# Expert weights in 1 MB transfers: splitting every refill of a ring in two

## The chip, the cores and the metric

The kernel runs on one core of a Trainium2 chip. Its time is device microseconds of one execution; the median of three runs of the kernel before is 2060.9 us (2057.89 to 2061.14). Weights and activations are float32.

## The reference, cut to what matters

Two blocks are applied to 256 tokens of width 1024. The first mixes a long convolution and a gated recurrence and ends in a retrieval of single-neuron experts. The second has two layers, each with attention (or spatial gating) and then sixteen experts of which each token takes two. The change lies in the experts of the two layers:

```
def expert_block(args):
    xblk, e = args
    return (jax.nn.silu(xblk @ w_gate[e]) * (xblk @ w_up[e])) @ w_down[e]
```

with `w_gate`, `w_up` and `w_down` of 1024 x 1024 float32 for each of 16 experts: 12 MiB an expert, 192 MiB a layer, all of it read once.

## The kernel before

The program is a row of stages: `front_stage` (the first block), `gating_stage` (layer 0's mixing), `moe_stage` for layer 0, `dilated_stage` (layer 1's attention) and `moe_stage` for layer 1. What matters here is `moe_stage`.

The sixteen experts are taken as eight pairs, and one pair is a visit. A visit of TensorE packs the tokens of the pair's two experts (up to 64 each), multiplies by gate (two halves of the columns), up (two halves) and down (two halves), and scatters the result back into PSUM. The two experts share the 128 rows of the output: expert j of the pair writes rows 64 j to 64 j + 63. Each of the six steps has a contraction of eight chunks of 128, and its weights come in two pieces of four chunks. So a visit takes 12 pieces (`HALVES`), and a layer 96. One piece is 128 partitions x 16 KB = 2048 KB (2.097 MB), and holds for both experts four chunks by 512 columns. TensorE does 16 matmuls of 512 columns on it.

The pieces live in a ring of 12 slots (`MOE_SLOTS`, `AHEAD`, `RING`). The first eleven are loaded during the stage before, the twelfth at the start of `moe_stage`. All others are refills: piece s goes into slot s mod 12 when TensorE has finished with piece s - 12. SP issues them all, in the order of use, from `load` (line 2558): it waits for `s_step`, which TensorE raises by one after the last matmul of every piece (line 2686), and calls `moe_load` (line 2459), which issues the transfer (line 2463). Each slot has a semaphore in `s_w`; TensorE waits for it ahead of the first matmul of a piece (`step`, line 2679). All transfers of SP stand in one hardware queue.

`IN_TWO` is the number of the first piece that comes in two transfers: chunks 0 and 1 of the piece (`QUARTER` = 2) in the first, 2 and 3 in the second, each with 8 KB of contiguous bytes for each partition. The second half has semaphores of its own, `s_w_rest`, for which TensorE waits in the middle of the piece (line 2681). Before, only the last eight pieces of a layer do so.

Behind the last piece SP issues the parameters of the closing norm and, in layer 0, three weights of the next stage (`w_v`, `w_k`, `w_in1`, line 2586); the first thing that TensorE does with them is `value_job` (line 2010 in the rows), at the end of layer 0's stage. All loops over visits are unrolled; a second pass, for experts with over 64 tokens, is a loop that is skipped when no expert has so many. The eighth visit is a function of its own (`visit_last`), behind a value that is loaded at run time. The semaphores of a stage are cleared by GpSimd at the start of the next (`clear_stale`).

Of the kernel before, what the change touches and what calls it, by code (L numbers as in the profile page):

```python
# [25 lines left out]
DC = D // P  # L26
# [1965 lines left out]
def dilated_weights(K):  # L1992

    return [K.cut(moe_base(K, slots), P, DC, w) for slots, w in ((3, N_DH * HD), (5, N_DH * HD), (7, N_DH * HD + MEM_W))]
# [451 lines left out]
HALVES = 2 * len(MOE_STEPS)  # L2446
# [7 lines left out]
def moe_slot(K, i):  # L2454

    return K.cut(moe_base(K, i + 1), P, DC // 2, 2, 512)


def moe_load(K, sp, layer, i, pair, chunks=slice(0, DC // 2)):

    name, h = MOE_STEPS[i // 2]
    src = K.dram[name][layer * NE + pair * 2 + h:layer * NE + pair * 2 + h + 1, :, i % 2, :]
    return sp.dma_start(moe_slot(K, (pair * HALVES + i) % MOE_SLOTS)[:, chunks],  # L2463
                        src.rearrange("o p (c j n) -> p (o c) j n", j=2, n=512)[:, chunks])


def moe_stage(K, layer):
# [9 lines left out]
    def sem(name):  # L2477
        return K.sem(f"moe{layer}_{name}")

    C = PACK_ROWS  # L2480
    PAIRS = NE // 2
    STEPS = MOE_STEPS
    NS = len(STEPS)
    AHEAD = MOE_SLOTS
    LAPS = [len(range(k, PAIRS * HALVES, AHEAD)) for k in range(AHEAD)]
    IN_TWO = PAIRS * HALVES - 8
    QUARTER = DC // 4

    at = Room(moe_base(K, AHEAD), ROUTE_COLS + 2 * T + 2 * MEM_W)
# [17 lines left out]
    FIRST_FREE = PAIRS * HALVES - (AHEAD - 3)  # L2507

    s_w = K.s_moe_w
    s_w_rest = [sem(f"w{s % AHEAD}_rest_in") for s in range(IN_TWO, PAIRS * HALVES)]  # L2510
    s_par, s_np, s_cols = K.lasting_sem(f"moe{layer}_params_in"), sem("passes"), sem("norm_columns_in")
    s_pk, s_pg, s_xm, s_xe, s_step, s_sg, s_h = (sem(n) for n in (
        "pack", "pack_gated", "xe_mm", "xe", "step_mm", "silu", "hidden"))
# [9 lines left out]
    def since(eng, s, count):  # L2523

        if not (isinstance(count, int) and count <= 0):
            eng.wait_ge(s, count)

    def visits(eng, body, prologue=None, behind=None):

        pairs = PAIRS - 1 if behind else PAIRS

        def one_pass(q, before_last=None):
            if prologue:
                prologue(q * PAIRS)
            for e in range(pairs):
                if before_last and e == pairs - 1:
                    before_last()
                body(q, e)  # L2540

        def load():
            eng.wait_ge(s_np, 1)
            loaded.append(eng.value_load(NPASS[0:1, 0:1], min_val=1, max_val=PASSES))  # L2544

        loaded = []
        one_pass(0, load)
        passes = loaded[0]
        with eng.If_ne(eng.lower_val(passes - 1), 0):
            with eng.Fori(1, passes) as q:  # L2550
                if behind:
                    behind(q - 1)
                one_pass(q)

    with nc.Block() as block:  # L2555
        @block.sync
        def _(sp):
            def load(q, e):
                for i in range(EARLY_SLOTS if isinstance(q, int) and e == 0 else 0, HALVES):
                    s = e * HALVES + i  # L2560
                    if isinstance(q, int) and s < AHEAD:
                        moe_load(K, sp, layer, i, e).then_inc(s_w[s], 16)
                        continue
                    used = s - AHEAD if s >= AHEAD else s + (LAPS[s] - 1) * AHEAD - PAIRS * HALVES
                    since(sp, s_step, q * (PAIRS * HALVES) + (used + 1))
                    if s < IN_TWO:
                        moe_load(K, sp, layer, i, e).then_inc(s_w[s % AHEAD], 16)
                    else:
                        moe_load(K, sp, layer, i, e, slice(0, QUARTER)).then_inc(s_w[s % AHEAD], 16)
                        moe_load(K, sp, layer, i, e, slice(QUARTER, DC // 2)).then_inc(s_w_rest[s - IN_TWO], 16)  # L2570

            if not last_layer:
                sp.dma_start(LNT, d["ln2_cols"]).then_inc(s_cols, 16)
            visits(sp, load)
            more = sp.value_load(K.NMORE[0:1, 0:1], min_val=0, max_val=PASSES - 1)
            sp.wait_ge(s_step, more * (PAIRS * HALVES) + (PAIRS * HALVES - (AHEAD - 1 - PARAM_SLOT)))
            sp.dma_start(LG, d["ln2_g"][layer].partition_broadcast(P)).then_inc(s_par, 16)
            sp.dma_start(LB, d["ln2_b"][layer].partition_broadcast(P)).then_inc(s_par, 16)

            if not last_layer:  # L2580
                steps = sp.value_load(NSTEPS[0:1, 0:1], min_val=FIRST_FREE, max_val=FIRST_FREE + (PASSES - 1) * (PAIRS * HALVES))
                names = ("w_v", "w_k", "w_in1")
                for n, (to, name, later) in enumerate(zip(dilated_weights(K), names, (0, 2, 4))):
                    sp.wait_ge(s_step, steps + later if later else steps)
                    src = d[name].rearrange("(c p) n -> p c n", p=P) if n == 2 else d[name][0].rearrange("p (c n) -> p c n", c=DC)
                    sp.dma_start(to, src).then_inc(K.s_att_w[n], 16)
            if last_layer:
                for t in range(TT):
                    sp.wait_ge(s_fin, t + 1)
                    sp.dma_start(K.out[t * P:(t + 1) * P, :], H[:, t, :]).then_inc(s_out, 16)  # L2590
                sp.wait_ge(s_out, 16 * TT)
# [61 lines left out]
        def _(te):  # L2653
# [19 lines left out]
            def step(q, e, i, operand, b, s_op, used, part=range(DC)):  # L2673

                for c in part:
                    s = e * HALVES + 2 * i + c // (DC // 2)
                    if c % (DC // 2) == 0:
                        te.wait_ge(s_op, used + (c // (DC // 2) + 1))
                        te.wait_ge(s_w[s % AHEAD], q * (LAPS[s % AHEAD] * 16) + (s // AHEAD * 16 + 16))
                    if c % (DC // 2) == QUARTER and s >= IN_TWO:  # L2680
                        te.wait_ge(s_w_rest[s - IN_TWO], q * 16 + 16)
                    for j in range(2):
                        x = pe.matmul(bank[b][j * C:(j + 1) * C, :], operand[:, c, j * C:(j + 1) * C],  # L2683
                                      RING[s % AHEAD][:, c % (DC // 2), j, :], start=(c == 0), stop=(c == DC - 1))
                    if c % (DC // 2) == DC // 2 - 1:
                        x.then_inc(s_step, 1)
# [15 lines left out]
            def gate_and_up(q, e):  # L2702
                n = q * PAIRS + e
                since(te, s_ye, n * 2)
                step(q, e, 0, XE, 0, s_xe, n * 2)
                if e:
                    te.wait_ge(s_pgt, n)
                    for h in range(2):
                        add_back(n - 1, h)
                step(q, e, 1, XE, 1, s_xe, n * 2)  # L2710
                since(te, s_pgt, n)
                since(te, s_ht, n * 2)
                for i in range(2, 4):
                    step(q, e, i, XE, i, s_xe, n * 2)
# [145 lines left out]
def moe_stage_0(K):  # L2860
    moe_stage(K, 0)


def moe_stage_1(K):
    moe_stage(K, 1)
# [195 lines left out]
```

## Time and profile before

| | |
|---|---|
| median of 3 runs | 2060.9 us |
| the profiled execution | 2064.71 us |
| its span (first to last instruction) | 2062.8 us |
| mean granted TensorE clock | 0.935 |
| TensorE busy | 1768.5 us (86%) |
| VectorE busy | 776.9 us (38%) |
| DMA | 761.82 MB, mean 369 GB/s |
| expert matmuls, L2683 | 3072, 680.3 us busy, 42.2 us idle before them |

A row "from-to" of the windows gives each engine's busy time with the number of instructions, then the granted clock, the mean share of the 16 DMA engines that is busy, and what they moved. In a row of the timeline the first number is the start, the second the length of a group of like instructions that follow on each other, and the bracket tells the idle time before it and what ended it. Since the ends of matmuls are modelled, gaps of some tenths of a microsecond are to be read as order, not as exact times. Layer 0's expert stage runs from about 1049 to 1483 us of the span, layer 1's from about 1619 us to the end.

### The profile page before, as it was taken

To read this page: it belongs to the slowest core of one execution; us is meant where nothing else is said; L and a number is where in the kernel's file an instruction comes from. 1 tells how busy PE (TensorE), PEld (TensorE's weight loads), DVE (VectorE), ACT (ScalarE), POOL (GpSimd) and SP (SyncE) were. 2 spreads that over 40 slices of the span, in tenths; PEclk is the share of its full clock that TensorE was granted. 3 is DMA by queue.
4 is the path that set the end of the run, shared out by engine and by line. 5 is a ranking of instruction groups with operands and counts; after the bars stand their busy time and mean duration, and the time that the engine had idled before them with its cause. 6 is when DMAs were issued, how large, how long until landed. Compare 5 with 4: busy or idle time off the path is not lost. (4 is left out here: it accounts for less than half of the span.)

```text
span 2062.8 us, 23546 instructions
## 1 busy us (share of the span) xinstructions
PE 1768.5 (86%) x9356; PEld 918.0 (44%) x9356; DVE 776.9 (38%) x1897; ACT 424.3 (21%) x1000; POOL 299.9 (15%) x284
## 2 busy tenths in 40 slices
PE   9999997876655665568999999988899999999887
PEld 7779873552321111124564444333377644433332
DVE  3945178776667777754230000000224300000002
ACT  2481122221221122223111101000223200000001
POOL 0000033543444444430000000000000000000000
PEclk9999998898887667889999999999999999999999
DMA  7237389999999999997789999999964999999997
GB/s 267 93 125 302 143 341 404 397 421 421 420 421 421 421 421 421 421 421 304 315 356 426 426 428 426 428 426 423 420 242 199 378 428 426 427 426 427 426 424 310
DMA packets 81710, 761.82 MB, mean 369 GB/s; under 512 B 9060, under 2 KB 10053, under 8 KB 18102
## 3 DMA queue, kind: packets, MB, share of 16 engines
q1 hardware_dynamic: 43926, 489.35, 56.9%
q0 software_dynamic: 37664, 270.84, 31.9%
q8 instruction: 78, 1.28, 0.2%
q14 instruction: 42, 0.34, 0.0%
HBM read 759.11 MB, written 1.05 MB: 369 GB/s over the span
## 5 line engine op out<-in xcount | busy, mean ns | idle before, releaser
L2683 PE MATMUL bank<-arena 128*64 128x512 f32 x3072 | 680.3, 597 | 42.2 <-DMA arena<-in_w_up 16.8
L1085 PE MATMUL bank<-arena 64*64 64x512 f32 x2032 | 320.4, 784 | 224.4 <-ACT arena L795 224.4
L2683 PEld LDWEIGHTS bank<-arena 128*64 128x64 f32 x3072 | 231.0, 137 | 477.5 <-issue 448.2
L588 POOL DMA_INDIRECT arena<-in_peer_uv,arena x256 | 288.5, 1127 | 614.2 <-PE bank L1085 301.0
L1458 DVE CUSTOM_DVE_ANT_0 arena<-arena 128x1024 f32<-128x1024 f32 x256 | 313.6, 1225 | 156.6 <-DMA arena<-in_peer_uv,arena 153.2
L2811 DVE TENSOR_TENSOR arena<-arena,bank 128x512 f32<-128x512 f32 x32 | 22.0, 687 | 705.7 <-PE bank L2683 705.7
L1085 PEld LDWEIGHTS bank<-arena 64*64 64x64 f32 x2032 | 92.6, 175 | 432.5 <-ACT arena L795 257.0
L844 PE MATMUL bank<-arena 128*128 128x272 f32 (+2 forms) x768 | 144.8, 349 | 0.2 <-ACT arena L614 0.2
L844 PEld LDWEIGHTS bank<-arena 128*128 128x128 f32 x768 | 126.2, 191 | 19.4 <-issue 2.5
L790 ACT ACTIVATE arena<-arena 128x4 f32<-128x4 f32 (+1 forms) x69 | 14.1, 205 | 465.0 <-DVE arena L1458 465.0
L1541 POOL DMA_DIRECT2D arena<-in_w_router x2 | 1.1, 574 | 566.0 <-POOLq L2555 531.3
L2616 ACT ACTIVATE arena<-bank 128x512 f32<-128x512 f32 x32 | 19.1, 597 | 277.9 <-PE bank L2670 165.1
L795 ACT ACTIVATE arena<-arena 128x64 f32<-128x64 f32 x256 | 68.6, 336 | 25.1 <-DVE arena L1476 25.1
L2610 ACT ACTIVATE arena<-bank 128x512 f32<-128x512 f32 x32 | 19.0, 595 | 240.9 <-PE bank L2692 240.9
L2625 ACT ACTIVATE arena<-bank 128x512 f32<-128x512 f32 x32 | 19.1, 597 | 216.7 <-PE bank L2683 216.7
L2670 PE MATMUL bank<-arena 128*128 128x512 f32 x128 | 59.7, 606 | 3.0 <-ACT arena L2625 3.0
L2661 PE MATMUL bank<-arena,h_res 128*128 128x128 f32 x512 | 62.1, 281 | 0.0
L2661 PEld LDWEIGHTS bank<-arena,h_res 128*128 128x128 f32 x512 | 60.9, 199 | 0.0
L1005 PE MATMUL bank<-arena 128*128 128x128 f32 x512 | 59.8, 275 | 0.0
L1005 PEld LDWEIGHTS bank<-arena 128*128 128x128 f32 x512 | 58.5, 192 | 0.0
L2229 PE MATMUL bank<-arena 128*128 128x256 f32 x224 | 51.2, 382 | 0.0
L2229 PEld LDWEIGHTS bank<-arena 128*128 128x128 f32 x224 | 41.6, 190 | 7.0 <-issue 1.3
(466 smaller groups left out, 1538.0 us busy)
## 6 DMA issues: line engine op xcount, KB each, us to landing
arena<-in_w_gate SPq DMA_DIRECT2D x64, 2048.0 KB, 32.3
arena<-in_w_up SPq DMA_DIRECT2D x56, 2048.0 KB, 32.4
arena<-in_w_down SPq DMA_DIRECT2D x56, 2048.0 KB, 33.2
arena<-in_w_in SPq DMA_DIRECT2D x13, 2048.0 KB, 8.2
arena<-in_w_up SPq DMA_DIRECT2D x16, 1024.0 KB, 38.8
arena<-in_w_down SPq DMA_DIRECT2D x16, 1024.0 KB, 27.0
arena<-in_w_out SPq DMA_DIRECT2D x2, 4096.0 KB, 18.2
arena<-in_wq SPq DMA_DIRECT2D x3, 2048.0 KB, 12.4
```

What stands on the lines that cost most here:

```text
L588: nc.gpsimd.indirect_dma_start(SLOT[slot_of[j]], None, d["peer_uv"], bass.IndirectOffsetOnAxis(IDX[:, u % 4, k:k + 1], 0)).then_inc(s_row[ ...
L795: a.activation(DIAG[:, k, :], DIAG1, ACT.Copy, scale=WGT[:, u, k:k + 1]).then_inc(s_diag, 1)
L844: m = pe.matmul(bank[n % 2][:, 0:w], RING[b % 2][:, c, q * P:(q + 1) * P], NT[:, c, lo:lo + w], start=(c == 0), stop=(c == DC - 1))
L1005: m = pe.matmul(bank[b][:, j * P:(j + 1) * P], WQ_CHUNK[k][c][:, j * P:(j + 1) * P], XT[t][:, c, :], start=(c == 0), stop=(c == DC - 1))
L1085: m = pe.matmul(bank[banks[t][half]][to:to + HALF, :], DIAG[lo:lo + HALF, k + j, :], row[lo:lo + HALF, D + half * 512:D + (half + 1) * 512 ...
L1458: v.tensor_tensor_reduce(SLOT[slot_of[j]][:, 0:D] if n == 0 else SCR, SLOT[slot_of[j]][:, 0:D], XF[u // PH], 1.0, 0.0, ALU.mult, ALU.add, ...
L2229: m = pe.matmul(b[:, 0:T], (WK if kind == "k" else WIN)[:, c, cols], XT[:, c, :], start=(c == 0), stop=(c == DC - 1))
L2616: a.activation(HID[:, b * 512:(b + 1) * 512], bank[b][:, :], ACT.Silu).then_inc(s_sg, 1)
L2661: x = pe.matmul(bank[c // 4][:, c % 4 * P:(c % 4 + 1) * P], H[:, t, c * P:(c + 1) * P], PK[:, t, :], start=(t == 0), stop=(t == TT - 1))
L2670: pe.matmul(bank[Y_BANKS[t][h]][:, :], PGT[:, t * P:(t + 1) * P], HID[:, h * 512:(h + 1) * 512], start=isinstance(n, int) and n == 0, stop ...
L2683: x = pe.matmul(bank[b][j * C:(j + 1) * C, :], operand[:, c, j * C:(j + 1) * C], RING[s % AHEAD][:, c % (DC // 2), j, :], start=(c == 0), ...
L2811: v.tensor_tensor(HID[:, cs], HID[:, cs], bank[2 + b][:, :], ALU.mult).then_inc(s_h, 1)
```

## The change

`IN_TWO` becomes 12: every piece from the thirteenth on (s >= 12, that is every refill) comes in two transfers of 1024 KB. The first twelve of each layer stay whole. The second halves get one semaphore for each slot, twelve instead of eight in a stage, and since a slot is now refilled in seven laps, TensorE waits for a count that grows by 16 with each lap.

```
-    IN_TWO = PAIRS * HALVES - 8
+    IN_TWO = AHEAD
...
-    s_w_rest = [sem(f"w{s % AHEAD}_rest_in") for s in range(IN_TWO, PAIRS * HALVES)]
+    s_w_rest = [sem(f"w{s}_rest_in") for s in range(AHEAD)]
...
                         moe_load(K, sp, layer, i, e, slice(0, QUARTER)).then_inc(s_w[s % AHEAD], 16)
-                        moe_load(K, sp, layer, i, e, slice(QUARTER, DC // 2)).then_inc(s_w_rest[s - IN_TWO], 16)
+                        moe_load(K, sp, layer, i, e, slice(QUARTER, DC // 2)).then_inc(s_w_rest[s % AHEAD], 16)
...
                     if c % (DC // 2) == QUARTER and s >= IN_TWO:
-                        te.wait_ge(s_w_rest[s - IN_TWO], q * 16 + 16)
+                        te.wait_ge(s_w_rest[s % AHEAD], q * ((LAPS[s % AHEAD] - 1) * 16) + s // AHEAD * 16)
```

## Rows read from the trace of the kernel before

**Rows 1.** The page's 40 equal slices of the span (51.6 us each).
```profile
DMA  7237389999999999997789999999964999999997
GB/s 267 93 125 302 143 341 404 397 421 421 420 421 421 421 421 421 421 421 304 315 356 426 426 428 426 428 426 423 420 242 199 378 428 426 427 426 427 426 424 310
```

**Rows 2.** The chain of waits from 1000 us on: start, us, what.
```profile
1708.53 13.97 PE bank L2683 x64
...
1759.54 13.97 PE bank L2683 x64
...
1883.91 49.00 DMA arena<-in_w_gate
...
1942.24 49.61 DMA arena<-in_w_gate
...
2020.21 27.67 DMA arena<-in_w_down
```

**Rows 3.** Timeline of TensorE in layer 1's seventh visit, whole pieces (start, us, what).
```profile
1952.76 3.65 PE L2683 MATMUL bank<-arena 128*64 128x512 f32 x16 [0.40 <-DMA arena<-in_w_up]
...
1967.47 3.65 PE L2683 MATMUL bank<-arena 128*64 128x512 f32 x16 [1.25 <-DMA arena<-in_w_up]
```

**Rows 4.** Windows: whole pieces in the first row, halves in the other two.
```profile
1650.00:1850.00 200.00, 196.94 (x952) 80.55 (x950) 11.33 (x39) 19.78 (x36) 0.00 (x0) 1.00 1.01 427
1438.00:1466.00 28.00, 27.05 (x126) 8.90 (x122) 2.67 (x4) 2.07 (x4) 0.00 (x0) 1.00 1.01 419
2008.00:2022.00 14.00, 14.00 (x68) 4.66 (x66) 0.69 (x1) 0.60 (x1) 0.00 (x0) 1.00 1.01 421
```

**Rows 5.** Timeline of SP's queue in layer 1: its first refills.
```profile
1628.64 10.63 SPq L2463 DMA_DIRECT2D arena<-in_w_gate  x4
```

**Rows 6.** Line 2463 from 1550 us on: all its expert loads, issue to landing.
```profile
DMA to landing us min/median/max: 7.1/32.8/51.6
```

**Rows 7.** Timeline of TensorE in layer 1's last visit, halves.
```profile
2006.86 19.26 PE L2683 MATMUL bank<-arena 128*64 128x512 f32 x88
2026.65 1.94 PE L2683 MATMUL bank<-arena 128*64 128x512 f32 x8 [0.53 <-DMA arena<-in_w_up]
...
2036.56 1.94 PE L2683 MATMUL bank<-arena 128*64 128x512 f32 x8 [0.46 <-DMA arena<-in_w_down]
...
2045.54 1.94 PE L2683 MATMUL bank<-arena 128*64 128x512 f32 x8 [0.67 <-DMA arena<-in_w_down]
2047.92 1.94 PE L2683 MATMUL bank<-arena 128*64 128x512 f32 x8 [0.44 <-DMA arena<-in_w_down]
```

**Rows 8.** Timeline of TensorE: end of layer 0's seventh visit, last visit, `w_v`.
```profile
1417.02 3.65 PE L2683 MATMUL bank<-arena 128*64 128x512 f32 x16 [0.54 <-DMA arena<-in_w_down]
1424.46 8.78 PE L2683 MATMUL bank<-arena 128*64 128x512 f32 x32 [3.79 <-issue]
...
1456.56 1.94 PE L2683 MATMUL bank<-arena 128*64 128x512 f32 x8 [0.45 <-DMA arena<-in_w_up]
...
1464.15 1.94 PE L2683 MATMUL bank<-arena 128*64 128x512 f32 x8 [0.29 <-DMA arena<-in_w_down]
1466.54 1.94 PE L2683 MATMUL bank<-arena 128*64 128x512 f32 x8 [0.45 <-DMA arena<-in_w_down]
...
1471.15 7.32 PE L2683 MATMUL bank<-arena 128*64 128x512 f32 x32
...
1487.85 5.43 PE L2010 MATMUL bank<-arena 128*128 128x384 f32 x16 [2.23 <-DMA arena<-in_w_v]
```

**Rows 9.** Windows: the gather of the first block.
```profile
500.00:900.00 400.00, 240.90 (x1412) 86.19 (x1410) 286.49 (x668) 85.19 (x258) 179.42 (x157) 0.79 1.01 421
```

**Rows 10.** SP's issues, ns min/median/max: room in the queue; then layer 1's end.
```profile
L2463 SPq DMA_DIRECT2D arena<-in_w_down x4: 327/328/328, 1142.2 to 1152.5; - x4
L2463 SPq DMA_DIRECT2D arena<-in_w_down x8: 2129/2140/3832, 2001.6 to 2020.2; - x8
```

**Rows 11.** DMA issues of the page: KB each, median us from issue to landing.
```profile
arena<-in_w_down SPq DMA_DIRECT2D x16, 1024.0 KB, 27.0
```

## The prediction

> **What bounds the kernel now.** I read the page's slices first [rows 1]. In the two expert stages (slices 22 to 29 and 33 to 39) the DMA engines are busy for nine tenths or more, at 420 to 428 GB/s. TensorE is busy for 86% of the whole span, so the shares alone don't say which of them sets the end. The chain of waits does [rows 2]: from 1883.9 us on it consists of two spans of 49.0 and 49.6 us on a `w_gate` transfer and one of 27.7 us on a `w_down` transfer, between them only a little TensorE work, which ends as TensorE starts on the last half piece. Before 1883.9 us the chain is TensorE's own, since eleven pieces lie ready when the stage starts. TensorE takes 51.0 us for a visit of twelve pieces (1708.53 to 1759.54 in the same rows), while the DMA engines need 12 x 4.9 = 58.9 us for twelve, with 4.9 us from the spacing below. So TensorE gains some 8 us on the transfers in every visit, eats up the ring, and in the sixth visit starts to wait.
>
> The spacing: where TensorE waits for whole pieces it restarts at 1952.76 and, three pieces later, at 1967.47 us [rows 3], 4.90 us for each, though the work on one takes 3.65 us. One piece is 2048 KB or 2.097 MB; at 4.905 us that is 427.5 GB/s, which agrees with the 427 GB/s of a long stretch [rows 4]. The DMA share there is 1.01: all 16 engines are full, nothing idles between transfers.
>
> Does this bind from the first refill to the end? SP issues the first refill of layer 1 at 1628.64 us [rows 5] and TensorE starts on the last half piece at 2047.92 us [rows 7]: 419.3 us for 84 pieces. 84 x 4.905 is 412.0 us. The missing 7 us are the start from an empty queue (the shortest time from issue to landing in this stage is 7.1 us [rows 6], 2.2 us more than one piece takes) and hold-ups of single engines. One of these can be seen: from 2036.56 to 2045.54 us three half pieces land in 8.98 us, 3.0 us each, where the next is 2.4 behind [rows 7]. So the stage's end is first refill + 84 pieces x time of one + a fixed tail of some 15 us, and what the change does to the time of a piece counts in full.
>
> **What the change does.** Pieces 12 to 87 of each layer (76 of the 84 refills) become two transfers of 1024 KB with rows of 8 KB per partition instead of one with rows of 16 KB; the first twelve and the last eight stay as they are. It removes no byte, no matmul and no wait.
>
> *Time of a transfer.* The last eight pieces of either layer already run in this form, so its price stands in the trace. In layer 0 TensorE restarts on a half at 1456.56 and, four landings later, at 1466.54 us [rows 8]: 2.495 us for each, 4.99 us for a piece. In layer 1 it is 2026.65 to 2036.56 us [rows 7]: 2.478, or 4.955 for a piece. The DMA rate over stretches with only such transfers in them is 419 and 421 GB/s beside 427 for whole pieces, at the same DMA share of 1.01 [rows 4]; with 420 that gives 2.097/0.420 - 2.097/0.427 = 0.08 us more per piece (0.07 to 0.09 by the two). The restarts give 0.05 and 0.085. A third witness from another queue: the gather of the first block, in 8 KB rows too, runs at 421 GB/s [rows 9]. I take 0.08 us. 76 x 0.08 = 6.1 us for a layer, 12.2 us for both; the bounds are 2 x 76 x 0.05 = 7.6 and 2 x 76 x 0.09 = 13.7 us.
>
> The Trainium skill would give other sums. "SBUF — State Buffer", section "The DMA setup-cost knee", puts a 1 MiB transfer at 341 GB/s because each pays some 2 us of its own; I weigh it as a rival below. "DMA: Bandwidth & Descriptors", section "Why small descriptors are slow", names about 3 cycles per packet on the engine's internal bus. Eight packets more per engine and piece at the 850 MHz that the page gives for the fabric would be 0.03 us, an estimate of some 4 us for the whole change: a third of what the trace shows for the same step.
>
> *SP.* 152 more transfers to issue. One takes 0.33 us of SP in a stretch where the queue has room [rows 10], two 0.66 us, against one piece released per 3.5 us at TensorE's fastest: hidden. Later the queue is full and an issue of a half is held for 2.1 us, most of the time of one landing [rows 10]. The median from issue to landing is 32.8 us over all loads of layer 1 and 27.0 us for the halves of `w_down` [rows 6, 11], so with halves less lies in the queue, but still some ten transfers (27.0/2.49). It doesn't run dry. Behind the blocked SP wait only the norm parameters and, in layer 0, `w_v`, `w_k` and `w_in1`, which stand in the same queue behind the pieces anyway.
>
> *TensorE.* It gets 76 waits in a layer in the middle of pieces, each ahead of a matmul. Their price where they are already satisfied: from 2006.86 us 88 matmuls run in 19.26 us over three such waits [rows 7], 0.219 us each, and 64 without any take 13.97 us [rows 2], 0.218 each. So nothing. Where they aren't satisfied, TensorE starts a piece one half landing (2.5 us) earlier, finishes it some 1.8 us earlier (half of the 3.65) and releases its slot that much sooner; SP is blocked then and the queue full, so the next landing is not moved. Behind TensorE's wait stand ScalarE's and VectorE's steps of the visit, which only come when the pieces do.
>
> *What is late next.* At the end of layer 0 TensorE is close to even with the transfers: it waits 0.29 and 0.45 us on the halves of one piece, runs the last two pieces in one go (32 matmuls from 1471.15 us), and then waits 2.2 us for `w_v`, which stands behind the last piece in the queue [rows 8]. With every landing 6 us later both are late by 6 us; TensorE, which doesn't get slower, has 6 us of slack in this visit. From there to layer 1's first refill the order is TensorE's own and shifts as a whole. In layer 1 it waits before each of the last two halves (0.67 and 0.44 us), so the later landings pass on entirely.
>
> *Four semaphores more in a stage* are cleared by GpSimd at the start of the next, which is otherwise idle there: nothing.
>
> **Sum.** The profiled execution is 2064.7 us (span 2062.8 and 1.9 around it), 3.8 above the median of the three timed runs. It would become 2064.7 + 12.2 = 2076.9; the median 2060.9 + 12.2 = 2073.1, 0.6% slower.
>
> **Rivals.**
> 1. *The rate of 419 to 421 GB/s belongs to the end of a layer and not to the size* (parameters and other small queues run there). Then 1 MB transfers in the middle of a layer run at 427 and nothing changes: 2061. For it: all direct rows come from the ends. Against it: the rate is down from the first half piece on, and the gather of another stage has it.
> 2. *The finer grain gains* (the other side). The place is the border from the seventh to the last visit: the seventh ends on a piece that TensorE waited for (1417.02 us, 3.65 us of work [rows 8]); with halves it would end 1.8 us sooner, then comes a gap of 3.79 us and the last visit, in layer 0 with hardly a wait. If the last visit is TensorE's there, 1.8 us are gained in each layer: 2060.9 - 3.6 = 2057.3. It decides only if the halves cost less than 1.8/76 = 0.024 us a piece; the rows say three times that, and the waits of 0.29 to 0.67 us in both last visits say that the landings rule.
> 3. *Extra hold-ups.* More transfers and instructions bring more delays like the 1.5 us (8.98 less 3 x 2.49) in [rows 7]. They add up where they hit the engine that is already last. Two more in each layer: 2060.9 + 12.2 + 6 = 2079.
> 4. *Each half pays its completion anew.* If the 2.2 us of start (7.1 less 4.9) came with each of the 152 additional transfers, it would be 334 us: 2395. The halves in [rows 7, 8] that land 2.4 to 2.5 us apart, with all 16 engines full, speak against it. By the 341 GB/s of the Trainium skill ("SBUF — State Buffer", same section) a piece would take 6.15 us and the kernel an estimated 190 us more; the 419 to 421 GB/s of [rows 4] are this very size, so the trace disagrees: transfers that stand in a queue don't pay it one by one.
> 5. *The small price only* (some 4 us, 2065): a cost per packet less than what the ends show.
>
> **How the numbers follow.** My forecast has 82%. Rival 1 has 5%, rival 2 3%, rival 3 7%, rival 4 1%, rival 5 2%. What a measurement of this kernel can tell from no change is about 0.2%, 4 us, so below 2056.8 is faster and above 2065.0 slower. The forecast, rivals 3 and 4 and half of rival 5 are slower: 91%; rival 1 and half of rival 5 are the same, and I leave rival 2 its 3% for faster: 6% and 3%. The range goes from the lower bound, 2060.9 + 7.6 = 2068.5, less 1 for the spread of the three runs (2057.9 to 2061.1), to the upper, 2060.9 + 13.7 = 2074.6, plus two extra hold-ups of 1.5: 2067.5 to 2077.6.
>
> **What would show it.** Right: about 420 GB/s through both expert stages at a share of 1.01; TensorE's waits in the sixth and seventh visit in halves, 2.49 us apart; the first refill of layer 0 at the same time as now, that of layer 1 some 6 us later, the last half landing some 12 us later; the first wait for a transfer in a layer earlier than now. Wrong: 427 GB/s with 8 KB rows (rival 1), a last visit with no wait for a transfer (rival 2), stretches below 410 GB/s or a DMA share under 1.0 between refills (rivals 3 and 4).

## The result and the profile after

The changed kernel takes 2074.16 us in the median (2071.93 to 2078.91) against 2060.9 us; the ratio is 1.0062 with a 95% interval of 1.0047 to 1.0077, so it is slower by 10 to 16 us. Forecast were 2073.1 us and a range of 2067.5 to 2077.6.

First two windows of the kernel after, one in the middle of each layer; the second is the first stretch of [rows 4]. The columns are PE, PEld, DVE, ACT and POOL busy, then granted clock, DMA share and GB/s.

```profile
1100.00:1280.00 180.00, 177.46 (x842) 70.65 (x844) 9.71 (x31) 16.22 (x30) 0.00 (x0) 1.00 1.01 420
1650.00:1850.00 200.00, 196.94 (x952) 80.70 (x950) 11.35 (x39) 19.78 (x36) 0.00 (x0) 1.00 1.01 420
```

The same stretch of layer 0 in the kernel before:

```profile
1100.00:1280.00 180.00, 177.01 (x840) 70.22 (x838) 9.17 (x31) 16.62 (x30) 0.00 (x0) 1.00 1.01 427
```

Where the kernel before moved 427 GB/s at a DMA share of 1.01 (this row and [rows 4]), this one moves 420 at the same share. The DMA engines are as full as before and get less done.

The stages' ends, from SP's and TensorE's timelines of the kernel after: the first refill of layer 0, the first matmul on `w_v`, the first refill of layer 1, and the last matmuls of layer 1 (L2670, the scatter of the last result).

```profile
1056.72 11.40 SPq L2463 DMA_DIRECT2D arena<-in_w_gate  x8
...
1492.14 5.43 PE L2010 MATMUL bank<-arena 128*128 128x384 f32 x16 [0.77 <-DMA arena<-in_w_v]
...
1629.75 11.10 SPq L2463 DMA_DIRECT2D arena<-in_w_gate  x8
...
2057.92 1.98 PE L2670 MATMUL bank<-arena 128*128 128x512 f32 x4 [0.70 <-ACT arena L2625]
```

The same four points of the kernel before: 1058.61 and 1628.64 us for the refills, 1487.85 us for `w_v` [rows 8], and for the end

```profile
1058.61 10.63 SPq L2463 DMA_DIRECT2D arena<-in_w_gate  x4
...
2050.55 1.98 PE L2670 MATMUL bank<-arena 128*128 128x512 f32 x4 [0.70 <-ACT arena L2625]
```

From first refill to `w_v`, layer 0 takes 1492.14 - 1056.72 = 435.4 us after and 429.2 before: 6.2 more. From first refill to the last matmuls, layer 1 takes 428.2 after and 421.9 before: 6.3 more. These two spans, called S0 and S1 from here on, are the best measure in the study, since what lies outside of them varies from execution to execution. They come from one profiled execution of each kernel. The example is the profiled pair itself: the execution after has a span of 2070.2 us, only 7.4 above the one before, because its first refill came 1.9 us earlier, and the way from `w_v` to layer 1's first refill took 137.6 instead of 140.8 us. 12.5 - 1.9 - 3.2 = 7.4.

### The profile page after: what moved, and what is told of

Read it like the earlier page. It is cut to its first block and busy times, and to the rows that moved or that the text cites. A ratio compares the mean times of both kernels' runs of the same rounds, so it can differ in the third digit from the quotient of the medians.

```text
span 2070.2 us, 23702 instructions
## 1 busy us (share of the span) xinstructions
PE 1766.3 (85%) x9356; PEld 905.1 (44%) x9356; DVE 776.8 (38%) x1897; ACT 424.3 (20%) x1000; POOL 296.6 (14%) x284
## 5 line engine op out<-in xcount | busy, mean ns | idle before, releaser
L2683 PE MATMUL bank<-arena 128*64 128x512 f32 x3072 | 688.3, 598 | 48.0 <-DMA arena<-in_w_up 16.3
L2683 PEld LDWEIGHTS bank<-arena 128*64 128x64 f32 x3072 | 226.2, 137 | 496.2 <-issue 427.8
L2670 PE MATMUL bank<-arena 128*128 128x512 f32 x128 | 59.7, 607 | 3.0 <-ACT arena L2625 3.0
```

What stands on the lines that cost most here:

```text
L2670: pe.matmul(bank[Y_BANKS[t][h]][:, :], PGT[:, t * P:(t + 1) * P], HID[:, h * 512:(h + 1) * 512], start=isinstance(n, int) and n == 0, stop ...
```

## Experiments

Each is a change to the kernel before unless it says otherwise, timed beside it on the same chip; the kernel before has 2062.0 and 2062.8 us there (12 and 20 runs).

### Same transfers, shorter rows

The theory: each row (one contiguous run for one partition) costs an engine something on top of its bytes. The rival: each transfer or semaphore does. The change doubles all of them. This one doubles the rows alone, by laying the halves of a piece apart in DRAM. (The first twelve pieces of a layer, which the expectation leaves as they were, get the shorter rows too; they lie ahead of both spans.)

```
-    return sp.dma_start(moe_slot(...)[:, chunks], src.rearrange("o p (c j n) -> p (o c) j n", ...)[:, chunks])
+    return sp.dma_start(slot.rearrange("p (a c) j n -> p a (c j n)", a=2), K.dram[name][row, :, :, i % 2, :])
...
-        return a...reshape(2 * NE, P, 2, DC * 512)
+        a = a...reshape(2 * NE, P, 2, 2, DC * 256)
+        return a.transpose(0, 1, 3, 2, 4)
```

> The kernel before, with the expert weights laid out in DRAM so that pieces 12 to 87 still come in one transfer of 2 MB with one semaphore, but in two runs of 8 KB for each partition instead of one of 16 KB; the last eight in two transfers as before. Theory (the size of the rows costs: every 8 KB run takes an engine a little longer than half a 16 KB run): the same 0.08 us per piece as the change, 420 GB/s in both expert stages, first refill to last half start in layer 1 about 425 us instead of 419.3, the whole about 2060.9 + 12 = 2073. Rival A (the number of transfers and semaphores costs): 427 GB/s, 2061. Rival B (half and half): 423 to 424 GB/s, 2067.

Measured: ratio 1.0064 (1.0044 to 1.0084). Two windows:

```profile
1290.00:1430.00 140.00, 118.41 (x554) 47.76 (x552) 6.60 (x23) 11.39 (x22) 0.00 (x0) 1.00 1.01 420
1650.00:1850.00 200.00, 196.94 (x952) 80.69 (x950) 11.34 (x39) 19.78 (x36) 0.00 (x0) 1.00 1.01 420
```

A group of its transfers on the page (count, KB each, median us to landing):

```profile
arena<-in_w_gate SPq DMA_DIRECT2D x64, 2048.0 KB, 32.2
```

And the timeline at the ends of both stages:

```profile
1056.74 10.84 SPq L2466 DMA_DIRECT2D arena<-in_w_gate  x4
...
1492.45 5.43 PE L2010 MATMUL bank<-arena 128*128 128x384 f32 x16 [2.09 <-DMA arena<-in_w_v]
...
1630.05 7.41 SPq L2466 DMA_DIRECT2D arena<-in_w_gate  x3
...
2059.07 1.99 PE L2672 MATMUL bank<-arena 128*128 128x512 f32 x4 [0.70 <-ACT arena L2627]
```

All pieces but the last eight of a layer are single transfers of 2048 KB again, and yet the rate is the changed kernel's 420 GB/s and the spans are S0 = 435.7 and S1 = 429.0, against 435.4 and 428.2. The whole of the loss comes with the rows; the 152 additional transfers, their issues and semaphores and TensorE's waits add nothing that these spans show. This also ends the rival that the lower rate belongs to the end of a layer.

### The change in layer 1 alone

```
-    IN_TWO = AHEAD
+    IN_TWO = AHEAD if last_layer else PAIRS * HALVES - 8
```

(on the changed kernel, with the count of the wait to match)

> The change in layer 1 alone; layer 0 as before. Theory (76 x 0.08 in each layer, passed on in full): half of the 12: 2060.9 + 6 = 2067; layer 0 at 427 GB/s and 429 us from its first refill to the matmuls that wait for w_v, layer 1 at 420 GB/s and 425.5 us from first refill to last half. Rival (layer 1's slack hides it, all comes from layer 0): 2061. Rival (all comes from layer 1): 2073.

Measured: ratio 1.0036 (1.0015 to 1.0056), 7 us. One window in each layer, then the timeline at the ends:

```profile
1290.00:1430.00 140.00, 124.04 (x594) 51.42 (x594) 7.00 (x24) 13.04 (x24) 0.00 (x0) 1.00 1.01 427
1860.00:2000.00 140.00, 121.46 (x554) 44.98 (x551) 6.36 (x22) 11.14 (x21) 0.00 (x0) 0.99 1.01 420
```

```profile
1059.78 10.63 SPq L2463 DMA_DIRECT2D arena<-in_w_gate  x4
1488.88 5.43 PE L2010 MATMUL bank<-arena 128*128 128x384 f32 x16 [0.76 <-DMA arena<-in_w_v]
...
1626.49 11.28 SPq L2463 DMA_DIRECT2D arena<-in_w_gate  x8
...
2054.92 1.98 PE L2670 MATMUL bank<-arena 128*128 128x512 f32 x4 [0.70 <-ACT arena L2625]
```

S0 is 429.1 us, as before the change, S1 428.4, as after it. The two layers add up. It also tells how well a span repeats: two executions with the same layer 0 differ by 0.1 us (429.2 and 429.1), two with the same layer 1 by 0.3 (428.17 and 428.43).

### How the cost goes with the rows: 4 KB

A version of the changed kernel with four transfers of 512 KB for each piece, which would have changed rows and transfers together, gave no result. This one changes the rows alone: one transfer for each piece, in four runs of 4 KB (32 rows for an engine and piece, where 16 KB rows make 8).

```
-    return sp.dma_start(slot.rearrange("p (a c) j n -> p a (c j n)", a=2), K.dram[name][row, :, :, i % 2, :])
+    return sp.dma_start(slot.rearrange("p c j n -> p c (j n)"), K.dram[name][row, :, :, i % 2, :])
```

(on the first experiment's kernel, with DRAM laid out to match)

> As the first experiment, but four runs of 4 KB for each partition and piece, in one transfer with one semaphore (the last eight in two transfers, of two runs each; here the first twelve too have such rows). Theory (a fixed cost for each row: 8 rows more per engine and piece cost 0.08 us, whatever their size): 24 rows more cost 0.24 us, 5.15 us per piece, 407 GB/s; over 84 pieces and two layers (84 x 0.24 less 8 x 0.08 that the kernel before pays already) x 2 = 39 us: 2062 + 39 = 2101. Rival (a step between 16 and 8 KB, nothing below): 420 GB/s, 2075. Rival (the cost grows faster than the number of rows): under 400 GB/s, over 2110.

Measured: ratio 1.0165 (1.0146 to 1.0184), 34 us. A window, then the timeline at the ends:

```profile
1290.00:1430.00 140.00, 118.89 (x576) 50.81 (x574) 7.69 (x25) 13.04 (x24) 0.00 (x0) 1.00 1.03 409
```

```profile
1057.80 7.41 SPq L2467 DMA_DIRECT2D arena<-in_w_gate  x3
...
1504.61 5.43 PE L2010 MATMUL bank<-arena 128*128 128x384 f32 x16 [0.77 <-DMA arena<-in_w_v]
...
1641.31 10.84 SPq L2467 DMA_DIRECT2D arena<-in_w_gate  x4
...
2081.18 1.98 PE L2673 MATMUL bank<-arena 128*128 128x512 f32 x4 [0.70 <-ACT arena L2628]
```

409 GB/s, S0 = 446.8, S1 = 439.9: 17.6 and 18.0 above the kernel before. The step from 16 to 32 rows costs (446.8 - 435.7)/84 = 0.13 us per piece or 8 ns a row, the step from 8 to 16 rows (435.7 - 429.2)/76 = 0.085 us or 11 ns a row (layer 1 gives 8 and 12 ns for the same steps). It is near to one price for each row, a little less for the shorter ones; I had set 10 ns throughout and so had expected 39 us more where 34 were measured. Between 16 and 4 KB there is no threshold.

### The other way: 32 KB

If a row costs, longer rows gain. The two pieces of a step lie next to each other in DRAM and, in the other order, in the ring; from piece 16 to 87 they come together, on one semaphore.

```
+    PAIRED = range(AHEAD + 4, IN_TWO)
...
+                    if s in PAIRED and s % 2 == 0:
+                        continue
                     since(sp, s_step, q * (PAIRS * HALVES) + (used + 1))
+                    if s in PAIRED:
+                        moe_load_both(K, sp, layer, i - 1, e).then_inc(s_w[s % AHEAD], 16)
```

> The kernel before, but pieces 16 to 87 come two at a time, in one transfer of 4 MB with one run of 32 KB for each partition (the two pieces of a step, laid side by side in DRAM); 12 to 15 whole, the last eight in halves. Theory (a fixed cost for each row; 16 KB rows still pay 0.08 us per piece for 8 rows): 32 KB rows save half of it, 0.04 us per piece, 72 x 0.04 = 3 us for a layer, 6 for both: 430 GB/s and 2055, if TensorE's wait for two pieces at once is made up before the last visit. Rival (16 KB rows are at the ceiling already, 427 GB/s): 2061. Rival (coarser transfers let the queue run dry at the start or make TensorE late at the last visit): 2063 or more, with waits of TensorE over 2 us at the pairs.

Measured: ratio 0.9971 (0.9958 to 0.9984), 6 us faster than the kernel before. A window, then the timeline at the ends and around the last visit of layer 1:

```profile
1650.00:1850.00 200.00, 197.02 (x935) 78.26 (x936) 11.92 (x40) 18.14 (x34) 0.00 (x0) 1.00 1.00 430
```

```profile
1055.49 10.63 SPq L2463 DMA_DIRECT2D arena<-in_w_gate  x4
1481.81 5.43 PE L2010 MATMUL bank<-arena 128*128 128x384 f32 x16 [1.65 <-DMA arena<-in_w_v]
1621.04 10.63 SPq L2463 DMA_DIRECT2D arena<-in_w_gate  x4
...
1957.38 8.67 PE L2699 MATMUL bank<-arena 128*64 128x512 f32 x32 [2.64 <-DMA arena<-in_w_up]
...
1987.84 8.78 PE L2699 MATMUL bank<-arena 128*64 128x512 f32 x32 [2.94 <-issue]
...
2032.47 7.09 PE L2699 MATMUL bank<-arena 128*64 128x512 f32 x32
2040.26 1.99 PE L2683 MATMUL bank<-arena 128*128 128x512 f32 x4 [0.70 <-ACT arena L2638]
```

430 GB/s; S0 = 426.3 and S1 = 419.2, 2.9 and 2.7 less than before. 2.9/72 = 0.04 us per piece for four rows saved: 10 ns a row once more. In the last visit of layer 1 no matmul waits for a transfer, it is TensorE's now, and waits of 2.6 us come in the visit before it, where TensorE needs both pieces of a transfer to start.

### The balance at the end

Pairs only up to piece 77, single pieces from there.

```
-    PAIRED = range(AHEAD + 4, IN_TWO)
+    PAIRED = range(AHEAD + 4, IN_TWO - 10)
```

> The version with rows of 32 KB, but only up to piece 77; from 78 on whole pieces, the last eight in halves. In the version before it TensorE waits 2.6 us for the second up pair of the seventh visit and runs the last visit with no wait for a transfer. Theory (TensorE has become the later one there by some 1 us): singles bring it 2 to 3 us forward in visit seven, the transfers take 10 x 0.045 = 0.5 us longer, the last halves are waited for again, and the whole is equal or up to 1 us less in a layer: ratio 0.996 to 0.997 to the kernel before, 2054 to 2055. Rival (the pairs cost nothing at the end, the singles only add rows): 0.5 to 1 us more than with pairs, 2056.

Measured: ratio 0.9966 (0.9952 to 0.9981), which its interval can't tell from the 0.9971. The spans: S0 = 1485.46 - 1059.07 = 426.4 and S1 = 2040.58 - 1622.16 = 418.4, together 0.7 us less than with pairs throughout, and the two halves of the piece before the last two are waited for again:

```profile
2025.56 1.94 PE L2699 MATMUL bank<-arena 128*64 128x512 f32 x8 [0.20 <-DMA arena<-in_w_down]
2027.96 1.94 PE L2699 MATMUL bank<-arena 128*64 128x512 f32 x8 [0.47 <-DMA arena<-in_w_down]
```

The last two pieces still run in one go, so the order of events is only in part the one expected, and the gain is too small for a claim. Either version is faster than both the kernel before and the changed one.

### Do the transfers set the end?

Half of the expert matmuls are left out (chunks 1, 3, 5 and 7 of every contraction).

```
                 for c in part:
...
+                    if c % 2:
+                        continue
```

> The kernel before without half of the expert matmuls: of the eight chunks of each contraction only chunks 0, 2, 4 and 6 are multiplied (L2683 has 1536 instead of 3072 matmuls); all transfers and waits stay. Theory (the transfers set the end of both expert stages): TensorE loses some 340 us of work, the time only what lies before the first refill and behind the last landing, some 1.8 us before and 1 to 2 us behind in each layer: 2062 - 6 = 2056; first refill to last half 417 to 419 us in layer 1; 427 GB/s. Rival (TensorE's pace of the first visits, 51.0 us each, is part of the sum): 100 to 300 us less.

Measured: one execution of 2053.8 us. The page's busy times, a window, and the timeline at the ends:

```profile
PE 1548.2 (75%) x7820; PEld 811.4 (40%) x7820; DVE 777.3 (38%) x1897; ACT 424.6 (21%) x1000; POOL 297.8 (15%) x284
```

```profile
1650.00:1850.00 200.00, 136.94 (x545) 53.91 (x545) 12.04 (x40) 18.58 (x34) 0.00 (x0) 0.86 1.01 427
```

```profile
1056.28 5.48 SPq L2463 DMA_DIRECT2D arena<-in_w_gate  x4
...
1484.13 5.43 PE L2010 MATMUL bank<-arena 128*128 128x384 f32 x16 [0.41 <-DMA arena<-in_w_v]
...
1620.03 3.76 SPq L2463 DMA_DIRECT2D arena<-in_w_gate  x3
...
2039.71 1.98 PE L2670 MATMUL bank<-arena 128*128 128x512 f32 x4 [0.70 <-ACT arena L2625]
```

TensorE is busy 220 us less and not the expected 340: half of the 680.3 us of expert matmuls would be 340, at the granted clock of 0.86 it is 396, and the trace has 451.6, so the clock explains about half of the difference. The spans are S0 = 427.9 and S1 = 419.7, only 1.4 and 2.2 below the kernel before. The transfers set the end, and TensorE's own pace in the first visits is no part of the sum. (The time itself is 9 us below the 2062.8 of the kernel before; about 5 of them lie outside of the two spans.)

### What the halves at the end are worth

No transfer is cut at all.

```
-    IN_TWO = PAIRS * HALVES - 8
+    IN_TWO = PAIRS * HALVES
```

> The kernel before with no transfer cut in two at all, the last eight included. Theory (halves cost 0.08 us per piece in the queue and gain only where TensorE waits for the last piece, half of its 3.65 us there): the last landing of a layer comes 8 x 0.08 = 0.6 us sooner; in layer 1 TensorE ends 1.8 - 0.6 = 1.2 us later, in layer 0 w_v comes 0.6 us sooner and is what TensorE waits for. Sum +0.6 us: no difference that can be measured, 2061 to 2063. Rival (the halves at the end are worth much more, some 2.5 us for each wait in the last visit): 2066 or more.

Measured: ratio 1.0004 (0.9993 to 1.0015). S0 = 1484.10 - 1055.36 = 428.7, 0.5 less than before; S1 = 2044.85 - 1621.68 = 423.2, 1.3 more. In layer 1 TensorE waits for the last whole piece and then has all 16 matmuls ahead of it:

```profile
2040.51 3.65 PE L2683 MATMUL bank<-arena 128*64 128x512 f32 x16 [0.74 <-DMA arena<-in_w_down]
```

So the halves are worth about 1.3 us at one place, the end of layer 1, cost 0.5 us in layer 0 (where `w_v` is now there before ScalarE's part, for which TensorE waits instead), and nothing of either can be seen in the time of the kernel. The single spans carry the hold-ups spoken of below with them, so the 0.5 and 1.3 are the right size rather than exact.

## Why the prediction was right

*Transfers bind from the first refill on.* Right, and now shown: with half the matmuls the spans stay within 2.2 us. The chain of [rows 2] alone would not have shown it. It was said to have only a little TensorE work between its transfers; the second of them ends at 1991.85 us (1942.24 + 49.61) and the third starts at 2020.21, with 28.4 us of other things between, 22.9 of them TensorE's work.

*The price of 0.05 to 0.09 us per piece, taken as 0.08.* It was read from the last eight pieces, sixteen transfers in a layer. Measured: (6.2 + 6.3)/152 = 0.082. That these rows come from the size and not from the place, which was the first rival, is shown by the 420 GB/s in the middle of both layers and by the first experiment. The forecast had left open whether rows or transfers cost; it needed only their sum. It is the rows.

*SP and TensorE pay nothing.* Right for the sum. Line 2463 in the changed kernel's layer 1 (from 1550 us on): issues of SP, ns min/median/max, and us to landing:

```profile
L2463 SPq DMA_DIRECT2D arena<-in_w_up x60: 328/2140/4278, 1578.1 to 2008.2; - x60
...
DMA to landing us min/median/max: 4.9/26.8/28.7
```

Half of these issues take 2.1 us or more, as in [rows 10], and a transfer lands 26.8 us after its issue instead of 32.8 [rows 6], so SP is blocked for most of the stage and about eleven transfers (26.8/2.49) lie in the queue. It costs nothing because the queue never runs dry: the rate has no dent.

*Finer grain gains nothing in the middle.* TensorE does start on halves. Its timeline in the seventh visit of layer 1, kernel after:

```profile
1959.50 1.94 PE L2683 MATMUL bank<-arena 128*64 128x512 f32 x8 [0.47 <-DMA arena<-in_w_up]
1962.09 1.94 PE L2683 MATMUL bank<-arena 128*64 128x512 f32 x8 [0.65 <-DMA arena<-in_w_up]
1964.49 1.94 PE L2683 MATMUL bank<-arena 128*64 128x512 f32 x8 [0.46 <-DMA arena<-in_w_up]
```

Two halves take 4.99 us (1959.50 to 1964.49), a whole piece took 4.90 [rows 3]. TensorE waits twice (0.65 and 0.46 us) instead of once 1.25 and is no further forward, since the landings rule.

*What is late next.* In layer 0 the last visit has the predicted slack (waits of 0.23 to 0.59 us return in it). In layer 1 I wrote that TensorE would wait before each of the last two halves as in [rows 7]; it doesn't (timeline of the kernel after):

```profile
1994.41 1.94 PE L2683 MATMUL bank<-arena 128*64 128x512 f32 x8 [0.46 <-DMA arena<-in_w_down]
2001.61 10.03 PE L2683 MATMUL bank<-arena 128*64 128x512 f32 x32 [5.26 <-issue]
...
2045.31 1.94 PE L2683 MATMUL bank<-arena 128*64 128x512 f32 x8 [0.46 <-DMA arena<-in_w_down]
...
2049.92 7.31 PE L2683 MATMUL bank<-arena 128*64 128x512 f32 x32
```

TensorE runs the last two pieces in one go. The waits in [rows 7] had come from a hold-up and were no property of the order: in the kernel before the three halves behind piece 93 took 1.5 us too long. Without one, four landings take 4 x 2.49 = 9.96 us, and TensorE comes to its last half 10.0 us after the one at 2045.31 (the last 8 of the 32 matmuls), so the two are even; [rows 8] show the same in layer 0. Counted from the first refill, the second half of piece 93 is used 7.6 us later than before (2045.31 - 1629.75 against 2036.56 - 1628.64), and the end comes 6.3 us later. By the landings in the trace the hold-up of the kernel before starts with the first half of piece 94, where the last of the 16 engines' parts comes 1.4 us late and stays so; the kernel after has one of 0.9 us that starts with the first half of piece 92, ahead of the 2045.31. The step "what is late next" was right in its sum and wrong in this detail, and luck has a part in how well the single spans agree with 6.1. Such hold-ups are one of the terms that I could only bound, and what causes them wasn't tried.

The gap ahead of the last visit is longer too, 5.26 us in layer 1 where the kernel before has 3.78:

```profile
1987.09 3.65 PE L2683 MATMUL bank<-arena 128*64 128x512 f32 x16 [0.55 <-DMA arena<-in_w_down]
1994.52 8.78 PE L2683 MATMUL bank<-arena 128*64 128x512 f32 x32 [3.78 <-issue]
```

That is no new cost of the waits. From the last landing that the seventh visit waits for to the start of the last visit it is 7.43 us before (1994.52 - 1987.09) and 7.20 after (2001.61 - 1994.41): the gap grew because the work behind that landing shrank from 3.65 to 1.94 us. What does cost a little is the clock behind the longer standstill: the first 32 matmuls take 10.03 us instead of 8.78. The visit is late by 1.0 us by it, and its next waits for transfers, in the down step, take this up.

*The profiled execution.* 2076.9 us was forecast, 2071.9 it was. The base was the mistake: I carried the 3.8 us by which the one profile before lay above its median into the forecast for the next. Two signs went wrong with it: layer 1's first refill came 1.1 us later and not 6, the end of the span 7.4 us later and not 12. The part that made it slow is not in the expert stages. One window of TensorE alone over the stretch from `w_v` to layer 1's first refill (busy, granted clock, DMA share, GB/s), of the kernel before:

```profile
1490.00:1628.00 138.00, 135.65 (x729) 0.96 0.63 259
```

and of the kernel after:

```profile
1490.00:1628.00 138.00, 134.62 (x739) 0.99 0.66 271
```

The clock was at 0.96 in the one and 0.99 in the other, and the stretch from `w_v` to the refill 3.2 us longer in the first. The same stretch took 137.6 us in three more of the profiled executions (1626.49 - 1488.88 in the one with layer 1 alone) and 135.9 to 139.2 in the other four, so the 140.8 of the kernel before are the odd ones.

*The rivals.* Rate by place: refuted (420 GB/s in mid-layer). Finer grain gains: refuted, by the price of the halves and by its mechanism. The seventh visit did end sooner behind its last landing, by 1.7 us, but the last visit started only 0.2 us sooner behind it (7.20 and 7.26 us in the two layers, 7.43 and 7.44 before), so cheaper halves wouldn't have brought the 1.8 us at this place either. More hold-ups: not seen, S0 and S1 grew by 6.2 and 6.3 and not by 9. A completion paid by each transfer: refuted; between the changed kernel and the first experiment, which have the same rows and 152 transfers of difference, S0 and S1 differ by less than 1 us. The small price only: refuted, 0.082 us is three times the 0.026 (4/152) that it needed.

For the price of a packet, here a row, the Trainium skill ("DMA: Bandwidth & Descriptors", section "Why small descriptors are slow (HBM only)") has about 3 cycles; at the 850 MHz that the page gives for the fabric that is an estimate of 3.5 ns. The runs here disagree: 8 to 12 ns for each row, at 4 to 32 KB. Its 341 GB/s for a 1 MiB transfer ("SBUF — State Buffer", section "The DMA setup-cost knee") is also not what a queue of such transfers shows here, which is 420.

## What to carry to other kernels

Where a full transfer queue sets the time, count rows, not transfers: cutting a transfer so that each partition's contiguous run is halved slows the whole stream, here by 1.7% (420 for 427 GB/s), while the earlier start that it buys was worth something here only at the very last piece. If the DRAM layout is yours, lay together what is loaded together; runs of 32 KB instead of 16 KB gave 0.3% here. And look for a place where a kernel already does what you think of: here the last pieces of the stream ran in the new form, and their spacing in the trace was the price.

## What was not expected of the hardware

The price of a row hardly depends on its length: 9 to 10 ns from 8 to 4 rows an engine (32 KB against 16 KB), 10 to 12 ns from 8 to 16, 8 ns from 16 to 32. Even runs of 16 KB are thus not at the ceiling. The packets' own times in the trace say the same: one of 16 KB takes 616.7 ns in the mean, one of 8 KB 315.0 (1300 to 1400 us of the kernels before and after), so two halves take 13 ns more than the whole.

Before the last visit TensorE stands still for a time that the weights don't explain (3.79 us in [rows 8], 5.26 us in the changed kernel's layer 1). When the visit starts goes by the last wait for weights of the seventh visit, and hardly by the work behind it: 7.1 to 7.5 us in both layers of the kernels before and after and of the ones with 8 KB rows, layer 1 alone, 4 KB rows, half the matmuls and no halves, with 1.9 to 3.7 us of matmuls in between. The trace has a candidate. In each of these stages, and in those with 32 KB rows, one packet of the queue called "instruction" (16 KB) starts about 3.5 us ahead of the visit's first matmul and ends 2.4 to 2.5 us ahead of it. The queues of the kernel after between 1994 and 2003 us (packets, MB, share):

```profile
q8 instruction: 1, 0.02, 0.8%
```

It goes from 1998.1 to 1999.2 us, and the first matmul is at 2001.61. So it looks as if TensorE waits for its program there. The last visit stands behind a value loaded at run time and a branch; whether they are the cause, and whether another order of the program would take the gap away, wasn't tried.

The first matmuls behind the gap are slow: 32 in 10.03 us, elsewhere in 7.09. A window of TensorE alone in the kernel after shows the granted clock at 0.50, the lower of its two levels (1.2 of 2.4 GHz), after the standstill:

```profile
2000.00:2005.00 5.00, 3.39 (x8) 0.50 1.01 416
```

With 32 KB rows this gap is on the path in layer 1, and it is the next thing to look at.
